# Recurrent steps of eight samples: states as the moving operand under 32 stationary columns, values spread from row groups

## The reference

```python
# gated delta rule (layer 0), L = 1
v_new = beta * (v - exp(g) * (k @ S))
o     = exp(g) * (q @ S) + (q . k) * v_new
S     = exp(g) * S + outer(k, v_new)
# gated linear attention (layer 1), L = 1
o = (q * exp(g)) @ S + (q . k) * v
S = exp(g)[:, None] * S + outer(k, v)
```

## Time and profile before

| | us |
|---|---|
| median of three runs | 2816.49 (2813.7 to 2823.06) |
| the profiled execution | 2824.7 |
| its span, first to last instruction | 2823.0 |
| PE busy | 2678.0 |
| DVE busy | 1435.8 |
| ACT busy | 1020.7 |
| PE's mean granted clock | 0.967 of full speed |

### The profile page before, as it was taken

One profiled execution on the slowest core, in us unless ns is written; L12 is line 12 of the kernel. 1 busy time (PEld: TensorE's weight loads), 2 busy tenths in 40 slices (PEclk: granted clock), 3 DMA queues, 4 the chain that ended last, 5 costly groups with the idle time before them and its releaser, 6 DMA issues.

```text
span 2823.0 us, 46989 instructions
## 1 busy us (share of the span) xinstructions
PE 2678.0 (95%) x20382; PEld 2354.7 (83%) x20382; DVE 1435.8 (51%) x2109; ACT 1020.7 (36%) x1517; POOL 312.0 (11%) x312
## 2 busy tenths in 40 slices
PE   7998887999998899999989999999999999999998
PEld 5677776877776677789979999998876788999997
DVE  6745665554354556356563445346556434533433
ACT  4323344342334345244332235144333323422323
POOL 2101002110000101014110001014101002100001
PEclk9998988999998999999999999999999999999999
DMA  5221111222321334322213334322243433333332
GB/s 160 68 84 61 39 39 53 61 61 68 97 83 54 92 89 136 93 72 76 75 53 98 91 92 135 95 71 75 75 129 110 127 94 95 113 96 91 90 92 74
DMA packets 424582, 243.86 MB, mean 86 GB/s; under 512 B 11494, under 2 KB 416349, under 8 KB 423856
## 3 DMA queue, kind: packets, MB, share of 16 engines
q1 hardware_dynamic: 424376, 240.85, 29.2%
...
## 4 chain that ended last, share of the span: by engine, by line
PE 75%; DVE 4%; ACT 3%; issue 2%; POOL 1%; DMA 1%; SPq 0%; POOLq 0%; ACTq 0%; DVEq 0%
PE ps L590 65%; PE ps L2416 1%; PE ps L2586 1%; PE ps L1231 1%; ACT window_b_scores L1770 1%; PE ps L2432 1%; ACT w_hi L508 1%; PE ps L2431 1%; PE ps L2579 0%; PE ps L2435 0%; PE ps L1560 0%; DVE w_lo L514 0%; PE ps L1744 0%; DMA ds_states<-state_dn 0%; PE ps L1736 0%
## 5 line engine op out<-in xcount | busy, mean ns | idle before, releaser
L508 ACT ACTIVATE w_hi<-w_raw 128x1024 fp32r<-128x1024 f32 x384 | 406.1, 1059 | 1214.4 <-PE ps L590 1196.4
L590 PE MATMUL ps<-act_hi,w_hi 128*128 128x260 f32 (+1 forms) x2688 | 754.6, 335 | 41.5 <-DVE w_lo L514 34.7
L590 PE MATMUL ps<-act_hi,w_lo 128*128 128x260 f32 (+1 forms) x2688 | 724.7, 324 | 0.0
L590 PE MATMUL ps<-act_lo,w_hi 128*128 128x260 f32 (+1 forms) x2688 | 723.2, 324 | 0.0
L514 DVE TENSOR_TENSOR w_lo<-w_raw,w_hi 128x1024 fp32r<-128x1024 f32 x384 | 480.3, 1251 | 173.5 <-ACT w_hi L508 173.4
L590 PEld LDWEIGHTS ps<-act_hi,w_hi 128*128 128x128 f32 x2688 | 453.6, 192 | 107.8 <-DVE w_lo L514 37.2
L590 PEld LDWEIGHTS ps<-act_hi,w_lo 128*128 128x128 f32 x2688 | 453.7, 192 | 41.3
L590 PEld LDWEIGHTS ps<-act_lo,w_hi 128*128 128x128 f32 x2688 | 454.1, 192 | 38.7 <-issue 3.5
L791 DVE TENSOR_TENSOR x<-x,ps 128x512 f32<-128x512 f32 (+1 forms) x160 | 110.5, 690 | 327.4 <-PE ps L590 327.2
L590 PE MATMUL ps<-op_hi_a,w_hi 128*128 128x512 f32 x640 | 267.4, 418 | 5.9 <-DVE w_lo L514 5.9
L590 PE MATMUL ps<-op_hi_b,w_hi 128*128 128x260 f32 x1280 | 260.1, 284 | 0.0
...
## 6 DMA issues: line engine op xcount, KB each, us to landing
w_raw<-mlp_w_up SPq DMA_DIRECT2D x128, 512.0 KB, 4.0
w_raw<-mlp_w_down SPq DMA_DIRECT2D x128, 512.0 KB, 3.8
...
x_store_b<-x SPq DMA_DIRECT2D x2, 2080.0 KB, 10.1
...
```

Of the source, the lines that this page charges most:

```text
L508: c.nc.scalar.activation(c.w_hi[:, slot], c.w_raw[:, slot], ACT.Copy).then_inc(c.hi_done, 1)
L590: last = t.matmul(c.ps[:, bank + i, 0:half.width], w[:, slot, k, :], x[:, k, half.cols(i)], start=(k == 0 and n == 0), stop=(k == KT - 1 a ...
```

## The change

Both sample phases are changed in the same way.

- The products with the states: the states become the moving operand (128 or 256 columns). The stationary operand is a block of 32 columns (`own`), zero but for the sample's own q (delta: q and k), cleared by memset and filled by eight small copies on DVE. The four heads go to four column groups, each with its 32 PSUM partitions, and all samples accumulate in one bank. The result has a row for each head and sample. ACT copies it out (`gathered`) and PE transposes it (`turned`).
- The values: kept as 32 columns per head (`v_cols`), transposed by PE, copied out by ACT (`v_rows`). To spread a sample's values, PE multiplies 8 rows of one row group with a column of the identity broadcast over 128 columns, one matmul per head (128 columns in delta, 256 in GLA). The heads write to different PSUM banks; where a bank comes again within a sample (`pair` in delta, `head` in GLA) PE waits for its own earlier matmul. The diagonals on DVE and the products with ones go.
- DeltaSamples has 13 steps in place of 12, GlaSamples 12 in place of 11.

```diff
--- before.py
+++ after.py
@@ -1489,22 +1489,26 @@
 class DeltaSamples(Phase):
 
 
+
+
     def __init__(self, c, area):
...
-        self.prod, self.tmp, self.vnew = (area(n, [P, HEADS, DEC]) for n in ("qk", "tmp", "v_new"))
-        self.diag = area("diagonals", [P, 2, HEADS, P])
+        self.prod, self.tmp = (area(n, [P, HEADS, DEC]) for n in ("qk", "tmp"))
+        self.own = area("own_columns", [P, DEC, HEADS, BLK])
+        self.v_cols, self.v_rows, self.gathered = area("v_cols", [P, HEADS, BLK]), area("v_rows", [P, P]), area("gathered", [P, P])
+        self.vnew = self.v_cols[:, :, 0:DEC]
...
         self.loaded, self.stored, self.tail_stored = c.sem("ds_loaded"), c.sem("ds_stored"), c.sem("ds_tail_stored")
-        self.paces = [4] * (4 + DEC)
+        self.paces = [4] * (5 + DEC)
 
     def over(self, eng):
         eng.wait_ge(*self.T.at("wide7"))
...
         for b in range(DEC):
...
         for b in range(DEC):
-            for h in range(HEADS):
-                u = b * HEADS + h
-                last = t.matmul(c.ps[:, 4, 128 + 2 * u:130 + 2 * u], self.states[:, u],
-                                proj[:, T_Q + h:T_K + h + 1:T_K - T_Q, SECOND.prompt + b], start=True, stop=True)
+            for h, blk in enumerate(BLOCKS):
+                last = t.matmul(c.ps[blk, 4, P:2 * P], self.own[:, b, h], self.states[:, b * HEADS + h], start=b == 0,
+                                stop=b == DEC - 1)
         last.then_inc(*self.T("mult"))
         yield
-        yield
+        pe.wait_ge(*self.S.at("gathered"))
+        t.transpose(c.ps[:, 4, 2 * P:3 * P], self.gathered[:], c.ident[:]).then_inc(*self.T("turned"))
+        yield
+        pe.wait_ge(*self.V.at("vnew"))
+        t.transpose(c.ps[:, 4, 3 * P:4 * P], self.v_cols[:].rearrange("p h n -> p (h n)"), c.ident[:]
+                    ).then_inc(*self.T("rows"))
+        yield
+        pe.wait_ge(*self.S.at("rows"))
         for b in range(DEC):
-            pe.wait_ge(*self.V.at(f"diag{b}"))
             if b >= 2:
                 pe.wait_ge(*self.V.at(f"new{b - 2}"))
-            else:
-                pe.wait_ge(*self.S.at("t2"))
-            t.matmul(c.ps[:, 5 + b % 2, :], c.ones[:], self.diag[:, b % 2], start=True, stop=True
-                     ).then_inc(*self.T(f"wide{b}"))
-            yield
+            for h, blk in enumerate(BLOCKS):
+                part, row = slice(blk.start, blk.start + DEC), blk.start + b
+                if h == 2:
+                    last.then_inc(*self.T(f"pair{b}"))
+                    pe.wait_ge(*self.T.at(f"pair{b}"))
+                last = t.matmul(self.wide(b, h), c.ident[part, row:row + 1].to_broadcast([DEC, P]), self.v_rows[part],
+                                start=True, stop=True)
+            last.then_inc(*self.T(f"wide{b}"))
+            yield
+
+    def wide(self, b, h):
+
+        return self.c.ps[:, 4 + 2 * (b % 2) + h % 2, h // 2 * P:(h // 2 + 1) * P]
 
...
         yield
-        yield
+        act.wait_ge(*self.T.at("mult"))
+        a(self.gathered[:], c.ps[:, 4, P:2 * P], ACT.Copy).then_inc(*self.S("gathered"))
+        yield
+        yield
+        act.wait_ge(*self.T.at("rows"))
+        a(self.v_rows[:], c.ps[:, 4, 3 * P:4 * P], ACT.Copy).then_inc(*self.S("rows"))
         yield
         act.wait_ge(*self.S.at("gates"))
-        act.wait_ge(*self.T.at("mult"))
         for b in range(DEC):
...
         c.delta["b"].over(dve)
+        v.memset(self.own[:], 0.0)
+        v.memset(self.v_cols[:], 0.0).then_inc(*did("zero"))
         v.tensor_tensor(self.prod[:], q, k, ALU.mult).then_inc(*did("prod"))
+        dve.wait_ge(*did.at("zero"))
+        for b in range(DEC):
+            both = proj[:, T_Q:T_K + HEADS, SECOND.prompt + b].rearrange("p (n h) -> p n h", h=HEADS)[:, 0:3:2]
+            last = v.tensor_copy(self.own[:, b, :, b:b + DEC + 1:DEC].rearrange("p h n -> p n h"), both)
+        last.then_inc(*did("own"))
         yield
...
         yield
-        dve.wait_ge(*self.T.at("mult"))
-        v.tensor_copy(self.both[:], c.ps[:, 4, 128:128 + 2 * HEADS * DEC]
-                      .rearrange("p (b h n) -> p b h n", b=DEC, h=HEADS)).then_inc(*did("both"))
+        yield
+        dve.wait_ge(*self.T.at("turned"))
+        turned = c.ps[:, 4, 2 * P:3 * P].rearrange("p (h c) -> p h c", h=HEADS)[:, :, 0:2 * DEC]
+        v.tensor_copy(by_head, turned.rearrange("p h (n b) -> p n h b", n=2)).then_inc(*did("both"))
...
-        v.tensor_tensor(self.vnew[:], x, self.tmp[:], ALU.subtract).then_inc(*did("v"))
+        v.tensor_tensor(self.vnew, x, self.tmp[:], ALU.subtract).then_inc(*did("v"))
...
-        v.tensor_tensor(self.vnew[:], self.vnew[:], beta, ALU.mult).then_inc(*did("vnew"))
+        v.tensor_tensor(self.vnew, self.vnew, beta, ALU.mult).then_inc(*did("vnew"))
...
-        v.tensor_tensor(self.prod[:], self.vnew[:], self.dots[:], ALU.mult).then_inc(*did("dv"))
+        v.tensor_tensor(self.prod[:], self.vnew, self.dots[:], ALU.mult).then_inc(*did("dv"))
...
         yield
-
-        def diagonal(b):
-            if b >= 2:
-                dve.wait_ge(*self.T.at(f"wide{b - 2}"))
-            v.tensor_tensor(self.diag[:, b % 2], spread(c.ident[:]), self.vnew[:, :, b:b + 1].to_broadcast([P, HEADS, P]),
-                            ALU.mult).then_inc(*did(f"diag{b}"))
-        dve.wait_ge(*did.at("vnew"))
-        diagonal(0)
         yield
         for b in range(DEC):
-            if b + 1 < DEC:
-                diagonal(b + 1)
             dve.wait_ge(*self.T.at(f"wide{b}"))
             dve.wait_ge(*self.S.at(f"decay{b}"))
...
-                last = v.scalar_tensor_tensor(out=self.states[:, u], in0=c.ps[:, 5 + b % 2, h * P:(h + 1) * P],
+                last = v.scalar_tensor_tensor(out=self.states[:, u], in0=self.wide(b, h),
                                               scalar=k[:, h, b:b + 1], in1=self.states[:, u], op0=ALU.mult, op1=ALU.add)
             last.then_inc(*did(f"new{b}"))
             yield
@@ -2511,25 +2531,27 @@
 class GlaSamples(Phase):
 
 
...
-        self.diag = area("diagonals", [P, 2, 2 * HEADS, P])
+        self.own = area("own_columns", [P, DEC, HEADS, BLK])
+        self.v_cols, self.v_rows, self.gathered = (area("v_cols", [P, 2, HEADS, BLK]), area("v_rows", [P, 2, P]),
+                                                   area("gathered", [P, 2, P]))
...
-        self.paces = [6] * (3 + DEC)
+        self.paces = [6] * (4 + DEC)
 
     def over(self, eng):
-        eng.wait_ge(*self.T.at("wide7"))
-        eng.wait_ge(*self.S.at("decay7"))
+        eng.wait_ge(*self.T.at("turned"))
+        eng.wait_ge(*self.S.at("gathered"))
         eng.wait_ge(*self.V.at("o"))
...
         c.gla["b"].over(pe)
         pe.wait_ge(*self.V.at("prod"))
-        t.matmul(c.ps[:, 4, 0:HEADS * DEC], c.ones[:], self.prod[:], start=True, stop=True).then_inc(*self.T("dots"))
-        yield
-        pe.wait_ge(*self.V.at("qe"))
+        t.matmul(c.ps[:, 5, 0:HEADS * DEC], c.ones[:], self.prod[:], start=True, stop=True).then_inc(*self.T("dots"))
+        pe.wait_ge(*self.V.at("v"))
+        for j in range(2):
+            last = t.transpose(c.ps[:, 6, j * P:(j + 1) * P], self.v_cols[:, j].rearrange("p h n -> p (h n)"), c.ident[:])
+        last.then_inc(*self.T("rows"))
+        yield
+        pe.wait_ge(*self.V.at("own"))
         pe.wait_ge(*self.V.at("dots"))
+        pe.wait_ge(*self.S.at("rows"))
         yield
         for b in range(DEC):
             part = b // 2
             if b % 2 == 0:
                 pe.wait_ge(self.loaded[part % 2], 32 * (part // 2 + 1))
                 for b2 in (b, b + 1):
-                    for h in range(HEADS):
-                        for j in range(2):
-                            col = 64 + (2 * h + j) * DEC + b2
-                            last = t.matmul(c.ps[:, 4, col:col + 1], self.unit(b2, h)[:, j * P:(j + 1) * P],
-                                            self.qe[:, h, b2:b2 + 1], start=True, stop=True)
+                    for h, blk in enumerate(BLOCKS):
+                        last = t.matmul(c.ps[blk, 4, 0:GDV], self.own[:, b2, h], self.unit(b2, h), start=b2 == 0,
+                                        stop=b2 == DEC - 1)
                 last.then_inc(*self.T(f"m{part}"))
-            pe.wait_ge(*self.V.at(f"diag{b}"))
             if b:
                 pe.wait_ge(*self.V.at(f"new{b - 1}"))
-            for m in range(2):
-                last = t.matmul(c.ps[:, 5 + (2 * b + m) % 3, :], c.ones[:], self.diag[:, b % 2, 4 * m:4 * m + 4], start=True,
-                                stop=True)
+            for h, blk in enumerate(BLOCKS):
+                part, row = slice(blk.start, blk.start + DEC), blk.start + b
+                if h == 3:
+                    pe.wait_ge(*self.T.at(f"head{b}"))
+                last = t.matmul(self.wide(b, h), c.ident[part, row:row + 1].to_broadcast([DEC, P]),
+                                self.v_rows[part].rearrange("p j n -> p (j n)"), start=True, stop=True)
+                if h == 0:
```

(47 more changed lines are left out.)

21 lines of the change are left out of this document (10 added, 11 removed).

## The result

| | before | after |
|---|---|---|
| median, us | 2817.89 (4 runs, 2813.7 to 2823.06) | 2798.74 (4 runs, 2795.75 to 2800.15) |
| ratio, with 95% interval | | 0.9923 (0.9909 to 0.9937) |
| span of the profiled execution | 2823.0 | 2798.4 |
| PE busy | 2678.0 | 2649.0 |
| DVE busy | 1435.8 | 1427.3 |

What follows compares the result with a forecast made beforehand. PE's own queue was taken to bound the kernel (busy 2678.0 of 2823.0 us). Terms -10.1 + 2.4 - 19.3 + 1.2 + 0.8 + 1.6 + (2.0 - 3.9 + 1.6) = -23.7 us: profiled 2801, median 2793, range 2781 to 2807.

Steps and rivals of the forecast that it cites:

- phases behind them: Layer 0 after delta: softmax waits unchanged, w_lo +2.0 us, scores wait near 4.4, finish factor wait gone, -3.9.
- finish of layer 1: Ln moves behind a tile's first split, +1.6 us (0 to 2.4); the 3.07 us wait for squares stays.
- rival (3): PE's wait for itself in the spreads costs 0.7 instead of 0.3 us, giving 2799; chance 0.12.
- the two large terms: Delta's products with the states, -10.1 us, and four GLA pairs' products and spreads, -19.3 us.
- Products: Products with the states: delta's 32 take 3.7 us instead of 13.7; a GLA pair's eight take 1.05.
- The trailing low level: Low clock for 2.8 us under dense matmuls behind delta's products, a loss of 1.4 us.
- Spreads: Spreading a sample's values: 1.15 against 0.86 us in delta, +2.4 for eight; 1.4 per GLA sample; self-wait 0.3.
- The beginning of the GLA phase: The first product (dots) waits for DVE, which now clears own_columns and v_cols before it: +1.2 us on PE.
- The state loads: GLA's loads for samples 4 to 7: PE waits some 0.8 us, twice, +1.6 (0 to 4).
- Groups taking turns: Rival: column groups stream one after another, 2828 us, slower; chance 0.03, and 0.03 with the clock up (2820).
- The low level as before: Rival: the clock falls in GLA and delta as before although groups overlap, 2804 us; chance 0.12.
- Moved phases that lose 11 us: Rival: one softmax wait of 7.6 us more and layer 0's finish unchanged, +11, 2804 us; chance 0.10.

Runs made afterwards that it cites:

- e1: Kernel before with only the delta samples changed as in the changed kernel; 2809.11 against 2821.59 us, ratio 0.9954.
- e5: The changed kernel measured again, unaltered, for comparison on the same chip; 2799.75 against 2823.20 us for the kernel before, ratio 0.9915.
- e7: Changed kernel, but in the GLA samples DVE forms q*k before the two memsets and PE's value transposes come one step later; 2789.21 us, one run.
- e8: Changed kernel with 7 instead of 6 k-steps after each of the last two GLA sample steps; 2789.35 us, one run.
- e6: Changed kernel with each head's delta spread in its own PSUM bank, so no self-wait within a sample; 2792.74 against 2823.20 us for before, ratio 0.9889.
- e4: Changed kernel with all products with the states in column group 0 (sample outputs wrong); 2812.34 against 2821.59 us for before, ratio 0.9973.
- e9: Changed kernel with four banks, q*k first, the 7-k-step pace, and state loads issued one step earlier; 2781.33 against 2821.09 us for before, ratio 0.9852.
- e3: Kernel before with one empty step at the end of each sample phase, nothing else; 2818.48 against 2821.59 us, ratio 0.9994.

## Why the prediction was right, and where only its sum was

The time came out inside the range, 5.7 us above the likeliest, and the profiled execution, forecast at 2801, took 2800.15: the profile of before lay 8 us above its median, that of after 1.4. By stretches the steps are off by more than their sum:

| stretch | forecast | measured in after |
|---|---|---|
| delta samples (-10.1 + 2.4 + 0.2) | -7.5 | -10.0 |
| phases behind them (0 + 2.0 - 3.9) | -1.9 | -6.6 |
| GLA samples (-19.3 + 1.2 + 0.6 + 1.6) | -15.9 | -13.3 |
| finish of layer 1 | +1.6 | +5.2 |
| sum | -23.7 | -24.7 |

(The forecast's 0.8 for transposes is split here. The measured sum is the -24.0 of the table above less the +0.7 of the run's beginning.) Four errors of -2.5, -4.7, +2.6 and +3.6 us cancel to 1. That the sum was hit is luck to that extent. A part of it is the luck of the profile, too: with the same delta code the first stretch is -8.3 and -8.2 in e1 and e5 and -11.9 and -11.6 in e7 and e8, the second -5.1 to -5.9. The median alone would not have told the forecast from rival (3), whose 2799 it is; e6 does. That the sign and the order of size were right is not luck, since the two large terms carried it.

**Products: right.** GLA: 1.00 us against the 1.05 taken, and no clock of 0.50 in any pair. Delta: 3.33 against 3.7. The trailing low level, for which 1.4 us had been set, was not there: the clock was back when the products ended. It is not always so, and not always down to begin with. In e1 and e5 the products took about 3.6 us at the low level, which there outlasted them by some 2.3 us, near the 2.8 forecast. In e7 and e8 they took 1.9 at the full one. The wait before them was 2.4 to 3.3 us in all of them. The whole stretch up to the end of the low level gained 9.8 us in e1 and e5, 11.6 in after and 13.2 to 13.4 in e7 and e8; the forecast's 10.1 lies among them.

**Spreads: right, within the bounds.** With the 0.1 in front, 1.19 us against 1.15 in delta and about 1.6 against 1.4 in GLA; e6 puts PE's wait for itself at 0.34 where 0.3 was taken. The way in and out is what was set too small: 0.21 was taken, and e6 has 0.54 - 0.21 = 0.33 and the 0.1 in front. In delta "a little for the second bank", 0.22 in that sum, made up for it; no run shows a cost of the bank apart from the wait. A GLA pair costs 4.17 against 3.85, so four save 18.0 and not 19.3 us. (The forecast's lower bound of 0.8 for delta should be about 1.3 by its own floor of 0.16.) The Trainium skill (TensorEngine Tiling (Array Packing), section Tiling Modes) has a change of tiling mode drain the array. In after the step that goes from column groups to row groups costs 2.49 = 1.00 + 1.49, and the step with row groups alone 1.48: the two differ by 1.01 us, in which the eight products lie. Two rounds of a single product of e4 (3.57 / 8 = 0.45) are 0.89, so about 0.1 us at most is left for the added switch and for what four groups cost beside one. The two cannot be told apart here, and 0.1 is what the forecast's 0.4 for four pairs had.

**The beginning of the GLA phase: right wait, wrong size.** The stall was foreseen, as 1.2 us. It is 1.85 against the 0.38 of before, 1.5 more, because q.k stands behind both memsets, which take 1.2 us on DVE (2060.45 to 2061.67), as forecast; the rest is that DVE starts the first memset about 0.25 us later, after the instruction in front of it, than it started its first copy before. What the forecast left out is that PE's idleness is followed by a low level: from 2062.6 to 2066 us the dense matmuls are 0.42 apart, about 1.5 us more. With 0.2 for the two transposes that is 3.2. e7 gave back 3.4 by the order alone, so both belong to the same stall.

**The state loads: right in sum.** 1.22 + 0.22 = 1.4 us against 1.6, in two waits as forecast, though not of 0.8 each; e9 takes them away.

**The phases behind, layer 0: the step that failed.** The four places of the softmax's blocks were counted rightly (k = 7, 1, 3, 5, four waits, 20.5 us against 18.9), and the wait of 2.4 for the factor went as forecast. What failed is the window samples. The prediction moved their scores from k = 1 to k = 5 and put w_lo at 2 us more, which was about right (1.6), but let the wait for the scores stay near 4.4, and it is 0.8: a wait at one place was priced by its own row at another. A wait of 1.4 us for ws_v_cache, which the profile of before also has and the prediction did not treat, is gone in after as well. All waits there go down by 5.7 us (29.0 to 23.3); some 1 us is left for the clock. e3 shows it with the old code: -6.3.

**The finish of layer 1: too small.** The factor's 1.65 us and the squares' 2.8 are as forecast. Not foreseen is w_lo, 0.90 + 3.11 where it was 0.8. The 3.11 come by way of SP: the reload of x waits in its queue for the finish's last splits, 17.4 us in both waits where it was 6.8, and the next weights are issued behind it. The prediction followed PE's next instruction and not SP's queue. e3 has 2.9 of it, with 19.3 us of SP's waits; in e8 and e9 these are 6.8 again and the wait is gone. The waits add 4.6, the rest is the clock. e8 shows that two k-steps more of pace undo it.

**The rivals.** Groups taking turns (2828) is refuted by the 1.00 us, and e4 prices its products: in turn, with the spreads still side by side, the kernel is 8 to 9 us faster than before. The rival's dearer spreads, 8 x 0.7 + 8 x 0.4 = 9 us, would bring that to no change, not to 11 us slower. It was priced too high: it kept the falls of the clock, left delta's products at 13.7 us where they take 7.1, and did not have layer 0's gain from the place. (Its pair also adds up to 7.6 us and not 7.8.) The low level as before (2804) is refuted by the windows: none in a GLA pair, and in delta it ended with the products. Dear self-waits (2799) are refuted by e6. Moved phases that lose 11 us (2804) are half true in layer 1 and the opposite in layer 0.
